# Decay rows of the gated DeltaNet layer: from TensorE transposes to transfers from DRAM

## The reference

```python
gc = jnp.cumsum(to_chunks(g, C, N), axis=-1)
diff = gc[..., :, None] - gc[..., None, :]
decay = jnp.where(tri, jnp.exp(jnp.where(tri, diff, 0.0)), 0.0)
lmat = jnp.where(strict, jnp.einsum('nbhik,nbhjk->nbhij', kb, kc) * decay, 0.0)
...
aqk = jnp.einsum('nbhik,nbhjk->nbhij', qc, kc) * decay
```

## Time and profile before

| | us |
|---|---|
| median of three runs (lowest, highest) | 2109.37 (2108.5, 2114.82) |
| the profiled execution's own time | 2113.68 |
| its span, first to last instruction | 2111.6 |
| TensorE busy | 2072.5 (98%) |
| VectorE busy | 997.2 (47%) |
| ScalarE busy | 697.7 (33%) |
| GpSimd busy | 454.6 (22%) |
| layer B's main loop, about | 1114 to 1650 |

### The profile page before, as it was taken

How to read it: one execution, slowest core, us unless ns; L and a number is a source line. 1 busy time by engine, 2 the same in 40 slices (tenths; PEclk the granted TensorE clock), 3 DMA queues, 4 the chain that set the end, 5 groups by cost and what they waited for, 6 DMA issues and landing times. The chain is left out here.

```text
span 2111.6 us, 36594 instructions
## 1 busy us (share of the span) xinstructions
PE 2072.5 (98%) x14446; PEld 1487.2 (70%) x14446; DVE 997.2 (47%) x2664; ACT 697.7 (33%) x1631; POOL 454.6 (22%) x639
## 2 busy tenths in 40 slices
PE   8999999999999999999999999999999999999998
PEld 6888888888888887555466777767666666665444
DVE  5234354354435345331238777777876133332252
ACT  4121321322131122231135555555564344532101
POOL 0522232222223213300023134322331200020000
PEclk9999999999999999999999999999998999999999
DMA  7411301211131127668412122222210461134451
GB/s 235 161 43 41 107 27 51 80 41 43 41 97 37 50 83 223 237 202 255 131 31 74 73 95 83 93 87 82 73 48 13 137 256 31 41 105 134 134 161 50
DMA packets 210238, 210.34 MB, mean 100 GB/s; under 512 B 14261, under 2 KB 181653, under 8 KB 209150
## 3 DMA queue, kind: packets, MB, share of 16 engines
q1 hardware_dynamic: 198070, 148.27, 23.7%
q0 software_dynamic: 12000, 59.73, 7.4%
HBM read 179.56 MB, written 68.23 MB: 117 GB/s over the span
## 5 line engine op out<-in xcount | busy, mean ns | idle before, releaser
L887 PE MATMUL bank<-arena 128*128 128x256 f32 (+1 forms) x2688 | 631.7, 386 | 0.0
L887 PEld LDWEIGHTS bank<-arena 128*128 128x128 f32 x2688 | 494.5, 190 | 75.3
L2104 PE MATMUL bank<-arena 128*128 128x352 f32 x1296 | 452.5, 470 | 0.1
L2104 PEld LDWEIGHTS bank<-arena 128*128 128x128 f32 x1296 | 220.8, 191 | 71.4 <-issue 1.0
L2909 PE MATMUL bank<-arena 128*128 128x352 f32 x576 | 176.4, 459 | 0.0
L3399 PE MATMUL bank<-arena 128*128 128x512 f32 x360 | 167.5, 599 | 0.0
L2162 PEld LDWEIGHTS bank<-arena 128*128 128x128 f32 x864 | 129.9, 194 | 45.7 <-DVE arena L2646 3.7
L2909 PEld LDWEIGHTS bank<-arena 128*128 128x128 f32 x576 | 106.6, 190 | 53.3
L1341 POOL TENSOR_TENSOR arena<-arena 128x272 f32<-128x272 f32 (+1 forms) x48 | 31.5, 656 | 507.4 <-ACT arena L1061 487.4
L2162 PE MATMUL bank<-arena 128*128 128x128 f32 x864 | 135.0, 280 | 1.5 <-DVE arena L2646 1.0
L1323 POOL TENSOR_TENSOR arena<-arena 128x512 f32<-128x512 f32 x96 | 122.8, 1279 | 11.3 <-POOL arena L1323 0.9
(11 more groups left out here) (432 smaller groups left out, 2754.1 us busy)
## 6 DMA issues: line engine op xcount, KB each, us to landing
arena<-in_w_in_a SPq DMA_DIRECT2D x48, 512.0 KB, 5.2
arena<-in_w_in_b SPq DMA_DIRECT2D x40, 512.0 KB, 7.5
arena<-in_cache_win_k SPq DMA_DIRECT2D x48, 256.0 KB, 6.1
arena<-in_cache_win_v SPq DMA_DIRECT2D x48, 256.0 KB, 4.7
out<-arena SPq DMA_DIRECT2D x40, 256.0 KB, 3.4
arena<-in_w_mem_kv SPq DMA_DIRECT2D x16, 512.0 KB, 8.1
arena<-in_cache_mem_k SPq DMA_DIRECT2D x32, 256.0 KB, 4.3
arena<-in_cache_mem_v SPq DMA_DIRECT2D x32, 256.0 KB, 4.2
```

The lines of the kernel that those rows point to most:

```text
L887: m = nc.tensor.matmul(o[:, 0:hi - lo], w, y, start=k == 0 and i in (0, 1, 3, 5), stop=k == KH - 1, skip_group_check=i in (2, 4, 6))
L2104: m = nc.tensor.matmul(bank[j % 3][:, 0:PART], ring.slots[:, (B1 + b) % RING, k, :], part_in(k, part_), start=k == 0, stop=k == KD - 1)
```

## The change

The cumulated decays gc of the prompt (128 x 64: 128 tokens of a chunk by 8 chunks x 8 heads) are transposed once, after "ra" of group 0, copied to SBUF and stored to a new DRAM tensor, gc_kept (64 x 128). From there SP loads, for each group 1 to 15, the four rows of 128 decays broadcast to all 128 partitions (256 KB), into one buffer at MQ[0]; the last group's go into xpad. The transfer for group G + 2 stands in SP's stream in iteration G and waits until the mask for group G + 1 has been added. In slot 5 VectorE adds the mask to the buffer's rows and writes ATs. The transposes "ra" of groups 1 to 15 and their PSUM bank are gone. SP's weight loads are put into the same stream in a new order, and four chain semaphores now belong to the phase and are cleared with it.

```diff
@@ SP @@
+        def rows_to(g):
+            h, c0 = g // 2, GR[g % 2][0]
+            sp.wait_ge(rows_away, 16)
+            after(sp, masked, g - 1)
+            if g == NG_ - 1:
+                sp.wait_ge(cvd, 3 * NG_)
+                sp.wait_ge(tap, 3 * (NG_ - 2))
+            src = gc_kept.rearrange("(c h) i -> h c i", h=HB)[h, c0:c0 + 4]
+            sp.dma_start(rows_of[g], src.unsqueeze(0).to_broadcast([P, 4, P])).then_inc(rows_in, 16)
+
+        def weights(b):
             if b % 3 == 2 and b // 3 >= 3:
                 state_away(b // 3 - 3)
             ring.load(sp, B1 + b + 1)
-        state_away(HB - 3)
-        ring.load(sp, B2 + RING)
+
+        for b in range(7):
+            weights(b)
+        readout(sp, 0, "gr")
+        sp.dma_start(gc_kept, gc_rows).then_inc(rows_away, 16)
+        rows_to(1)
+        for G in range(NG_):
+            if G % 2 and G < NG_ - 1:
+                weights(3 * (G // 2) + 8)
+                weights(3 * (G // 2) + 9)
+            if G + 2 < NG_:
+                rows_to(G + 2)
+            if G % 2 == 0:
+                weights(3 * (G // 2) + 7)
@@ buffers and order @@
+    gc_rows = r_sb[0:64, 1, :]
+    rows_of = [sb[:, MQ[0]:MQ[0] + 512]] * (2 * HB - 1) + [xpad[:, 1, 0:512]]
-    PREP = {5: ("ra",), 7: ("kt",), 8: ("kk",), 9: ("qk",), 15: ("vt",)}
-    NEXT = ("ra", "kk", "qk")
+    PREP = {7: ("kt",), 8: ("kk",), 9: ("qk",), 15: ("vt",)}
+    NEXT = ("kk", "qk")
+    AT_MASK = 5
@@ TensorE, once, behind turned(0, "ra") @@
+            o = bank_free(0, "gr")
+            nc.tensor.transpose(o[0:64, 0:P], gc[:, 0:64], ident).then_inc(wk, 1)
@@ ScalarE @@
+            if i == 0 and part_ == 0:
+                act.wait_ge(masked, NG_ - 2)
...
-            readout(act, G, "ra")
+            if G:
+                act.wait_ge(masked, G)
+            else:
+                readout(act, 0, "ra")
@@ VectorE @@
+            nc.vector.tensor_copy(gc_rows, b[0:64, 0:P]).then_inc(rd_dve, 1)
+
+        def mask_rows(G):
+            dve.wait_ge(rows_in, 16 * G)
+            if G > 2:
+                left(dve, G - 3, f"av{GR[(G - 3) % 2][1] - 1}")
+            nc.vector.tensor_tensor(ATs[G % 3], rows_of[G], wide4(mat(M_GE)), ALU.add).then_inc(masked, 1)
...
+                if s == AT_MASK and G + 1 < NG_:
+                    mask_rows(G + 1)
```

More of the change, by code:

```diff
@@ L115, with __init__ @@
 class Chain:
-    def __init__(self, nc, eng, name):
-        self.eng, self.sem, self.n = eng, nc.alloc_semaphore(name), 0
+    def __init__(self, sem, eng, name):
+        self.eng, self.sem, self.n = eng, sem(name), 0
     def __call__(self, ins):
@@ L158, in build @@
     part = dram("part", [2, SEQ, OW])
+    gc_kept = dram("gc_kept", [64, P])
     memT_kept = dram("memT_kept", [P, KD * NMEM])
@@ L525, in _ @@
     def _(dve):
-        own = Chain(nc, dve, "in_dve")
+        own = Chain(sem, dve, "in_dve")
         def norm(n):
@@ L1130, in _ @@
     def _(dve):
-        own = Chain(nc, dve, "dve_a")
+        own = Chain(sem, dve, "dve_a")
         def evacuate(t, i):
@@ L1300, in _ @@
     def _(pool):
-        own = Chain(nc, pool, "pool_a")
+        own = Chain(sem, pool, "pool_a")
         def weight_sums(pair, ns):
@@ L1747, in _ @@
     def _(dve):
-        own = Chain(nc, dve, "wa_dve")
+        own = Chain(sem, dve, "wa_dve")
         def add(n, half):
@@ L1930, in build @@
     vb = mv[:, 0:2, :].rearrange("p a b -> p (a b)").rearrange("p (c e) -> p c e", e=P)
+    rows_of = [sb[:, MQ[0]:MQ[0] + 512]] * (2 * HB - 1) + [xpad[:, 1, 0:512]]
+    rows_of = [w.rearrange("p (c e) -> p c e", e=P) for w in rows_of]
     flat = lambda v: v.rearrange("p a b -> p (a b)")
@@ L1980, in build @@
     reader_of = lambda n: "act" if n in ("ss", "ot") or n[:2] in ("qs", "tr") else "dve"
-    work = [(0, "ss"), (0, "ra"), (0, "kk"), (0, "qk")]
+    work = [(0, "ss"), (0, "ra"), (0, "gr"), (0, "kk"), (0, "qk")]
     for G in range(NG_ + 1):
@@ L2000, in build @@
     (pd, pr_, wk, rd_act, rd_dve, cvd, sild, sqd, hdv, hda, exd, mt0, onm, sqo, fac, tails, sqrt_o, cstep, xzero,
-     cvs, spread, base, tap, chosen) = (
+     cvs, spread, base, tap, chosen, rows_away, rows_in, masked) = (
         sem(f"b_{n}") for n in (
@@ L2005, in build @@
             "out_factors", "conv_tails", "out_roots", "conv_steps", "buffers_zeroed", "samples_convolved",
-            "diagonals_spread", "base_steps", "first_taps", "blocks_chosen"))
+            "diagonals_spread", "base_steps", "first_taps", "blocks_chosen",
+            "rows_kept", "rows_loaded", "rows_masked"))
     s_out = stored["state"]
@@ L2078, in state_away @@
             sp.dma_start(p_delta[0, 0, h], S_of(h, NT)).then_inc(s_out, 16)
-        for b in range(3 * HB):
+        def rows_to(g):
[8 more added lines that the diff above has]
+        def weights(b):
             if b % 3 == 2 and b // 3 >= 3:
@@ L2214, in chunk_step, with decay_rows @@
                 to(g, f"su{c}", [(kdec[:, c, :], vn[:, c % 2, :])])
+        def decay_rows():
+            o = bank_free(0, "gr")
+            nc.tensor.transpose(o[0:64, 0:P], gc[:, 0:64], ident).then_inc(wk, 1)
         def turned(G, name):
@@ L2283, in _ @@
         turned(0, "ra")
+        decay_rows()
         for u in units[PER_HEAD + KD:PER_HEAD + 2 * KD]:
@@ L2489, in _ @@
     def _(dve):
-        own = Chain(nc, dve, "b_dve")
+        own = Chain(sem, dve, "b_dve")
         stepped = [0]
@@ L2571, in turned, with decay_rows @@
                                         .to_broadcast([P, 4, P]), ALU.mult).then_inc(rd_dve, 1)
+        def decay_rows():
+            b = left(dve, 0, "gr")
+            nc.vector.tensor_copy(gc_rows, b[0:64, 0:P]).then_inc(rd_dve, 1)
[4 more added lines that the diff above has]
+            nc.vector.tensor_tensor(ATs[G % 3], rows_of[G], wide4(mat(M_GE)), ALU.add).then_inc(masked, 1)
         def matrix_step(G, s):
@@ L2772, in _ @@
     def _(pool):
-        own = Chain(nc, pool, "b_pool")
+        own = Chain(sem, pool, "b_pool")
         def prefix(h, i):
@@ L3009, in _ @@
     def _(dve):
-        own = Chain(nc, dve, "m_dve")
+        own = Chain(sem, dve, "m_dve")
         def conv_turned(t):
@@ L3487, in _ @@
     def _(act):
-        own = Chain(nc, act, "d_act_own")
+        own = Chain(sem, act, "d_act_own")
         def squared(o):
@@ L3558, in _ @@
     def _(dve):
-        own = Chain(nc, dve, "wb_dve")
+        own = Chain(sem, dve, "wb_dve")
         gt2 = lambda v: v[:, 64:66].unsqueeze(2)
```

## The result

The changed kernel takes 2160.93 us in the median of four runs (2159.60 to 2165.43), the kernel before beside it 2111.76 (2108.50 to 2114.82, four runs): a ratio of 1.0237, 95% interval 1.0212 to 1.0261. It is slower, and 2160.0 was forecast. The profiled execution took 2160.12 us, with a span of 2158.2, 46.6 us more than the 2111.6 of before.

The account below looks back on a forecast made before the run. TensorE, busy for 98% of the span, was taken as the bound. Late rows less gains made 32.2 us, half clock 18.0; these 50.2 on a median of 2109.4 gave 2160 us, range 2136 to 2177.

Parts of the forecast that it names:

- The gain of the transposes: TensorE, slot 5: dropping "ra" gains 0.44 us in iteration 1, 0.37 in each of 2 to 12, 0.1 in 14.
- The mask from SBUF: VectorE's masking add, reading two SBUF operands in place of one in PSUM: 0.01 us dearer, bounds 0 and 0.1.
- When the rows land: Row transfers of odd groups, behind the weight load and cache copy, land after some 41 us; even groups in time.
- Lateness: At the masks of groups 3, 5, 7, 9, 11 and 13: rows 5.4 to 6.7 us late, sum 36.8 us.
- The clock: TensorE behind each of six stalls: half clock loses 3.0 us each, 18.0 us in all; bounds 0 and 6.9 each.
- The mis-sized step: From the clock fall near 794 us: 5.9 us of resumed work at half clock, so 3.0 us lost per stall.
- The sum: Whole kernel: 32.2 us net of late rows and gains plus 18.0 of half clock, 50.2 us slower.
- The base: Starting time for the whole kernel: 2109.4 us, median of the runs before, to which 50.2 was added.
- rows in time: Rival: rows land within 34 us between mask and mask, nothing waits, gain 4.6 us, 2104.8 us; chance 0.08.
- The turn of 9 to 17 small pieces per packet: Skill page's DMA queue turns: 96 pieces on one engine would clear in 18 us, giving 2105; the prediction's trace disagreed.
- Late, but the clock stays up: Rival: rows late at the masks but TensorE's clock does not fall, 32.2 us slower, 2142 us; chance 0.12.
- Long half clock: Rival at the stalls: 13.8 us of half clock each, 41 us in all, or more rows late, 2183 us; chance 0.08.

Follow-up runs that it names:

- no_rows: The changed kernel without the row transfers of groups 2 to 15, the mask reading group 1's rows each time: 2107.59 us, ratio to before 0.9975.
- spread_copies: The changed kernel with each 2 MB cache copy issued as two 1 MB transfers of 32 pieces each: 2106.40 us, ratio to before 0.9969.
- two_buffers: The changed kernel with a second row buffer, so that rows are issued two iterations ahead: 2108.80 us, ratio to before 0.9982.
- busy_pe10: The changed kernel with 10 extra matmuls, output overwritten, ahead of x4's wait in the six iterations with late rows: 2152.52 us, ratio to before 1.0191.
- before_spread: The kernel before with its twelve 2 MB cache copies each cut into 2 x 32 pieces, nothing else: 2111.94 us, ratio to before 1.0000.
- spread_4: The changed kernel with each 1 MB row of the cache copies its own transfer, written as 4 pieces: 2108.64 us, ratio to before 0.9979.
- spread_late_mask: The changed kernel with cache copies in 32 pieces per row and slot 5's masking add moved behind base_turned: 2109.43 us, ratio to before 0.9985.
- two_spread: The changed kernel with both two row buffers and cache copies in 32 pieces per row: 2108.16 us, ratio to before 0.9972.

## Why the prediction was right

The time, 2160.0 forecast and 2160.9 measured, and the mechanism are right: six late rows at the groups named, none at the even ones, and half clock behind each. Two terms of the sum were off in opposite directions, and the base was low.

- **The gain of the transposes**: 4.6 us forecast; no_rows against before gives 4.1 between groups 2 and 15 and 0.1 ahead of them. x4 waits for base_turned from then on, 0.054 us between its end and x4's start, as in the earlier trace rows.
- **The mask from SBUF**: forecast 0.01 us dearer than 0.68; 691 ns in the median, against 678 before. No interval shows a cost of it.
- **When the rows land**: forecast 41 us for odd groups, measured 39.5 to 41.4. The third loads landed after 42.7 to 43.9 us (42.1 to 43.5 taken), the rows 0.84 to 0.87 us behind them (0.8 forecast). Rows of group 2 landed at 1155.35, 0.24 us before their mask started: as close as forecast. The rows of groups 4 to 12 that are even took 20.7 to 22.1 us. The reading that the copies land after 25 to 45 us took the record at its word; by the packets a copy lasts about 40 (see spread_copies). The forecast did not use the 25, since it went by the landings of the loads.
- **Lateness**: 36.8 us forecast, 41.0 measured. Loads that landed later make some 2.7 us of it (42.7 to 43.9 against the 42.1 to 43.5 taken, summed over six). The rest, some 1.5, is for the most part the gain itself, which I left out of this term: with iterations 0.35 us shorter the mask is reached that much sooner after the load is issued, and waits for it.
- **The clock**: 18.0 us forecast, 12.9 measured, 2.15 per stall in place of 3.0. The mis-sized step took the 5.9 us of half clock behind the resumption from the fall near 794 us. There, by that reading, the clock fell 0.9 us before work resumed. In these stops it fell 2.2 to 4.9 us before x4 started, so more of the 6.8 or 10.2 us of half clock lay in the stop, where it costs nothing: behind x4 there were 4.0, 3.4, 5.4, 4.3, 6.4 and 4.7 us, 28.1 in all, half of which is 14.1; in each interval the measured cost is 0.1 to 0.4 us under the half, and why is open.
- **The sum**: 36.8 + 18.0 - 4.6 = 50.2 forecast; 41.5 + 12.9 - 4.1 = 50.3 shown. That it fits to 0.1 us is luck: 4.7 too little, 5.1 too much, and 0.5 too much gain.
- **The base**: I added it to 2109.4, a median of three runs. In later runs before had medians of 2113.2 to 2113.6. On that base the forecast would have been 2163.6, and the distance measured about 47.5 us, 1.0225, in place of 49.2, so the hit to 0.9 us is luck as well; half clock near 1060 us and in iteration 13, in some executions and not in others, makes such differences of 3 us.
- **The rivals**: rows in time (2104.8) did not come about, and two_buffers, spread_copies and no_rows show what it would have been: ratios of 0.9969 to 0.9982, 3.8 to 6.6 us faster, around the 4.6 worked out. The turn of 9 to 17 small pieces per packet is refuted by the landings, as the 13 to 13 packets had said. "Late, but the clock stays up" was priced at 32.2 us over before; busy_pe10, which is this case made on purpose, has 39.3 by the medians. Its six stall intervals are 42.7 us longer than those of no_rows, which less the gain of 4.1 makes 38.6; the fall that stayed adds 1.5 in the profile. The lateness was under-priced here as in the forecast. Long half clock, 13.8 us behind each stall, did not come: each fall lasted 6.8 or 10.2 us, of which 3.4 to 6.4 lay behind x4's start.

## What to carry to other kernels

Before a wait is put on a transfer, look up how long its neighbours in the same stretch take to land, those above all that nobody waits for: they carry the warning. Here a copy of 2 MB from DRAM to DRAM in two rows held each load and row transfer over all partitions, issued while it ran, until about its own end. Two things took all of the harm away: to issue each row as a transfer of its own, written as 4 or 32 pieces, or to issue the small transfers a full copy's length earlier. A stall of TensorE of 6 to 8 us here costs about 2 us more in the half clock behind it; price that by how much of the fall lies behind the resumption.

## What the runs showed of the hardware

One transfer for each 1 MB row, in pieces, in place of one for two rows shortened a copy of 2 MB from about 40 us to 6 to 9 us, with packets of 65 KB in both and no loss to anything beside it (before_spread, 1.0000). Beside the slow form SP's queue moved one piece of 512 B per packet of 65 KB on the two engines, 12 to 12 in 14 us. When two such copies were in flight, the landing on record for the first, 24.5 us, was too early by some 17 us.

In single iterations of five runs there is a stop of 0.7 to 1.3 us in the middle of x4's 64 blocks, in which TensorE waits for nothing that the profile shows. TensorE's timeline in spread_4:

```profile
1499.81 0.56 PE L2211 MATMUL bank<-arena 32*32 32x16 f32 x45
1501.35 0.36 PE L2211 MATMUL bank<-arena 32*32 32x16 f32 x19 [0.98 <-issue]
```

In all eight such stops (two_buffers, spread_copies, spread_late_mask, spread_4 and two_spread) a transfer of 16 KB in the instruction queue had begun 1.0 to 1.8 us before; there are 42 or 43 of these transfers in 450 us, most without a stop behind them. That TensorE waits for code is an inference; no run tested it. The iteration is 0.9 to 1.5 us longer for it, in zero to two iterations of this stage in the profiled executions.
